# Encoder layer on one core: another tile order, squares ahead of high parts, and five smaller moves in the last two stages

## The reference

```python
o = rms_norm(o, sub_norm) * (1.0 - lam_init)
mix = jnp.concatenate([o_att * jax.nn.silu(g_att), o_lru * jax.nn.silu(g_lru)], axis=-1)
h = h + jnp.einsum('bsc,cd->bsd', mix, w_out[l])
e = jnp.einsum('bsp,pd->bsd', p[l], w_ple[l]) * jax.nn.sigmoid(jnp.einsum('bsd,de->bse', h, w_pg[l]))
h = h + rms_norm(e, g_ple[l])
```

## Time and profile before

| | us |
|---|---|
| times of three runs | 1026.09, 1027.68, 1029.20 |
| median | 1027.68 |
| profiled execution | 1027.9 |
| its span | 1026.1 |

### The profile page before, as it was taken

One profiled execution on the slowest core, in us unless ns is written; L12 is line 12 of the kernel. 1 busy time (PEld: TensorE's weight loads), 2 busy tenths in 40 slices (PEclk: granted clock), 3 DMA queues, 4 the chain that ended last, 5 costly groups with the idle time before them and its releaser, 6 DMA issues.

```text
span 1026.1 us, 15666 instructions
## 1 busy us (share of the span) xinstructions
PE 990.3 (97%) x5720; PEld 785.2 (77%) x5720; DVE 679.0 (66%) x1117; ACT 636.8 (62%) x1051; POOL 482.8 (47%) x396
## 2 busy tenths in 40 slices
PE   8999999999999999989999999999989999999996
PEld 7867777777788888878777777777767887777775
DVE  4735857592583341579999999999848672444444
ACT  7748485846631231569999999999737443444442
POOL 1163343626656540155677676665610125555451
PEclk9999999999999999999999999999989999999999
DMA  9741543323255437659867666523457780222221
GB/s 345 273 142 36 174 149 104 118 82 134 72 177 184 142 95 204 212 158 234 208 195 173 149 188 173 132 93 124 171 168 239 230 280 10 72 74 81 86 73 68
DMA packets 106909, 154.55 MB, mean 151 GB/s; under 512 B 10313, under 2 KB 69193, under 8 KB 106825
## 3 DMA queue, kind: packets, MB, share of 16 engines
q1 hardware_dynamic: 106688, 153.55, 50.0%
q10 hardware_dynamic: 144, 0.00, 0.0%
HBM read 104.17 MB, written 46.20 MB: 147 GB/s over the span
## 4 chain that ended last, share of the span: by engine, by line
PE 66%; DVE 17%; issue 10%; ACT 3%; POOL 2%; DMA 2%; DVEq 0%; POOLq 0%; SPq 0%; ACTq 0%
DVE E_ L1899 10%; PE b_ps L2340 6%; PE b_ps L2342 6%; PE b_ps L2341 6%; PE b_ps L2202 6%; PE b_ps L2204 5%; PE b_ps L2203 5%; PE o_ps L2397 3%; PE s_ps L2353 3%; PE w_ps L2314 3%; PE uT_ps L2277 2%; DVE ratio L1908 2%; PE left_ps L2527 2%; PE left_ps L2530 2%; PE left_ps L2529 2%
## 5 line engine op out<-in xcount | busy, mean ns | idle before, releaser
L1381 ACT ACTIVATE E_<-E_,nmax 128x1024 f32<-128x1024 f32 (+1 forms) x184 | 186.6, 1018 | 13.2 <-DVE nmax L1899 13.2
L1899 DVE CUSTOM_DVE_ANT_0 E_<-s_ps,bias 128x1024 f32<-128x1024 f32 (+1 forms) x184 | 188.2, 1057 | 9.2 <-PE s_ps L2353 9.0
L1087 POOL TENSOR_TENSOR E_<-E_,ratio 128x576 f32<-128x576 f32 (+3 forms) x92 | 84.7, 920 | 92.6 <-DVE E_ L1915 92.6
L1090 POOL TENSOR_TENSOR E_<-E_ 128x576 f32<-128x576 f32 (+3 forms) x92 | 103.6, 1126 | 7.2
L2204 PE MATMUL b_ps<-u_hi,wA_lo 128*128 128x512 f32 x256 | 99.8, 390 | 0.0
L2353 PE MATMUL s_ps<-KL,QL 128*128 128x512 f32 x256 | 88.6, 430 | 8.1 <-DVE nmax L1899 8.0
L1396 ACT ACTIVATE WT<-w_ps 128x1024 f32<-128x1024 f32 (+1 forms) x96 | 83.5, 870 | 5.9 <-PE w_ps L2314 5.5
L2314 PE MATMUL w_ps<-ident,E_ 128*128 128x128 f32 x624 | 83.5, 273 | 2.1 <-ACT WT L1396 2.0
L2202 PE MATMUL b_ps<-u_hi,wA_hi 128*128 128x512 f32 x216 | 85.5, 396 | 0.0
L2314 PEld LDWEIGHTS w_ps<-ident,E_ 128*128 128x128 f32 x624 | 72.5, 140 | 15.2 <-issue 6.3
L2203 PE MATMUL b_ps<-u_lo,wA_hi 128*128 128x512 f32 x216 | 84.1, 389 | 0.0
(11 more groups left out here) (345 smaller groups left out, 2595.8 us busy)
## 6 DMA issues: line engine op xcount, KB each, us to landing
QL<-qk_t SPq DMA_DIRECT2D x32, 256.0 KB, 7.2
KL<-qk_t SPq DMA_DIRECT2D x32, 256.0 KB, 8.5
bias<-line_d SPq DMA_DIRECT2D x8, 960.0 KB, 12.1
x_sb<-in_x SPq DMA_DIRECT2D x12, 512.0 KB, 9.0
z_ch<-z_stage SPq DMA_DIRECT2D x24, 256.0 KB, 3.2
qk_t<-qh SPq DMA_DIRECT2D x24, 256.0 KB, 2.3
qk_t<-ql SPq DMA_DIRECT2D x24, 256.0 KB, 2.8
mf<-mix_t SPq DMA_DIRECT2D x24, 256.0 KB, 4.8
```

Of the source, the lines that this page charges most:

```text
L1090: gp.tensor_tensor(one, one, two, ALU.add).then_inc(w_gp, 1)
L1381: act.activation(e, e, ACT.Exp, bias=nmax[:, n % 5, c:c + 1], scale=-1.0, accum_out=sums[:, n % 5, c:c + 1]).then_inc(e_done, 1)
L1899: dve.tensor_tensor_reduce(weights_at(n)[:, c, 0:n_tok], s_ps[:, c, 0:n_tok], b[:, ::-1], -1.0, 3e38, ALU.add, ALU.min, nmax[:, n % 5, c:c ...
```

## The change

It touches the tile loop and the pair loop alone.

- `SEQ`: tile 2 comes third and tile 8 fourth; `WHOLE` and `HALF` follow. Bank and waits are renumbered with it, and `add_x(3)` is done in two halves.
- SP: `load_o(2)` is issued ahead of the last `store_o`; in each step `load_mix(n + 2)` now stands ahead of `load_o(n + 3)`. The wait for the last `store_o` stands ahead of `load_o(3)`.
- ACT: in each step from the second on, `square_o(n + 3)` stands ahead of `mix_high(n + 1)`; `root_o` moves to just ahead of `scale_o` of the same tile. `gate_high` comes after both. The small instruction that had made the square root's table load early is dropped. The high parts of the embedding weights are made one step earlier.
- POOL: the first `wp_lo` ahead of the last `add_half`, the first three sums' low parts ahead of `p_low`.
- DVE: `mean_square(2)` ahead of `o_gate(1)`; `joined(g, 3)` ahead of `scaled_e(g, 1)`; in the last pair the multiplication by the gain writes to `sg` and needs only `e`, not its square, and the last additions are reordered.

```diff
-        SEQ = [0, 1, 8, 2, 9, 3, 10, 4, 11, 5, 6, 7]
+        SEQ = [0, 1, 2, 8, 9, 3, 10, 4, 11, 5, 6, 7]
...
             load_x_again(1)
+            load_o(2)
             store_o(1, HEADS // 2 - 1)
-            sp.wait_ge(o_st[1], 16 * 4)
-            load_o(2)
             load_mf(10)
             for n in range(NT):
+                if n + 2 < NT:
+                    load_mix(n + 2)
+                if n == 0:
+                    sp.wait_ge(o_st[1], 16 * 4)
                 if n + 3 < NT:
                     load_o(n + 3)
-                if n + 2 < NT:
-                    load_mix(n + 2)
...
             for k in range(1, len(HALF)):
+                if k == len(HALF) - 1:
+                    embedding_low(0)
                 add_half(k)
...
+            embedding_low(1)
...
+            sums_low(0)
             gp.wait_ge(fin["x_sum"], len(HALF))
             p_low(0, 1)
             p_low(0, 0)
-            sums_low(0)
...
             heads_out(2 * HEADS - 1)
+            square_o(2)
             mix_high(1)
-            act.activation(mse[:, 0:1], neghalf[:, 0:1], ACT.Sqrt, scale=-2.0)
-            square_o(2)
-            root_o(2)
...
             for n in range(NT):
+                if n == 0:
+                    root_o(2)
+                    scale_o(2)
+                if n + 3 < NT:
+                    square_o(n + 3)
                 if 1 <= n < NT - 1:
                     mix_high(n + 1)
-                if n + 2 < NT:
+                if 1 <= n < NT - 2:
+                    root_o(n + 2)
                     scale_o(n + 2)
-                if n + 3 < NT:
-                    square_o(n + 3)
...
             for g in range(PAIRS):
                 if g:
                     joined(g - 1, 3, "p2", right_ps[:], sg[0][:, LEFT])
+                    scaled_e(g - 1, 1)
                     gated_e(g - 1, 0)
...
                 a12_low(g + 1)
-                scaled_e(g, 1)
```

More of the change, by code:

```diff
@@ L459, in mix_bank @@
         def mix_bank(i):
-            if i < 3:
-                return (h_ps[:], hq_ps[:], all_ps[:, 4:8:3, :])[i]
+            if i < 4:
+                return (h_ps[:], hq_ps[:], h_ps[:], all_ps[:, 4:8:3, :])[i]
             return h_ps[:] if i % 2 else hq_ps[:]
@@ L1118, in add_half, with embedding_low @@
                                  ).then_inc(fin["x_sum"], 1)
+            def embedding_low(k):
+                gp.wait_ge(wp_hi_done, k + 1)
+                gp.tensor_tensor(wp_lo[:, k, :], wp_raw[:, k, :], wp_hi[:, k, :].bitcast(F32),
+                                 ALU.subtract).then_inc(wp_lo_done, 1)
             o_scale(0)
@@ L2010, in add_x @@
                     dve.wait_ge(fin[f"h_out{n % 2}"], 16 * min(n // 2, 4))
+                if n == 3:
+                    dve.tensor_tensor(h_sb[:, n, LEFT], mix_bank(n)[:, 0, :], row[:, LEFT], ALU.add)
+                    dve.tensor_tensor(h_sb[:, n, RIGHT], mix_bank(n)[:, 1, :], row[:, RIGHT], ALU.add
+                                      ).then_inc(fin["h_done"], 1)
+                    return
                 dve.tensor_tensor(h_sb[:, n % 4, :].rearrange("p (a b) -> p a b", a=2), mix_bank(n),
@@ L2063, in _ @@
             heads_scaled(2 * HEADS - 1)
+            mean_square(2)
             o_gate(1)
             mix_low(1)
-            mean_square(2)
             for n in range(NT):
@@ L2159, in half_gain @@
             def half_gain(k, r, c):
-                dve.wait_ge(fin["esq"], 2 * LAST + k)
-                dve.tensor_tensor(e_sb[:, r, c], e_sb[:, r, c], gpB[:, c], ALU.mult).then_inc(fin["t_done"], 1)
+                dve.wait_ge(fin["e_done"], START["e_done"] + 2 * LAST + k)
+                dve.tensor_tensor(sg[r][:, c], e_sb[:, r, c], gpB[:, c], ALU.mult).then_inc(fin["t_done"], 1)
             def last_mean(r, one, two):
@@ L2166, in last_mean, with last_sum @@
                                   ALU.add).then_inc(fin["ems"], 1)
-            def last_sum(r):
+            def last_sum(r, parts):
                 dve.wait_ge(fin["ers"], START["ers"] + 2 * LAST + r + 1)
-                for c in (RIGHT, LEFT):
-                    dve.scalar_tensor_tensor(out=e_sb[:, r, c], in0=e_sb[:, r, c], scalar=rse[:, r:r + 1],
+                for c in parts:
+                    dve.scalar_tensor_tensor(out=e_sb[:, r, c], in0=sg[r][:, c], scalar=rse[:, r:r + 1],
                                              in1=h_sb[:, slot_of(LAST, r), c], op0=ALU.mult, op1=ALU.add
@@ L2184, in _ @@
             dve.wait_ge(fin["t_done"], 2 * LAST + 3)
-            last_sum(0)
+            last_sum(0, (RIGHT,))
+            half_gain(4, 1, LEFT)
             last_mean(1, 1, 4)
-            half_gain(4, 1, LEFT)
+            last_sum(0, (LEFT,))
             dve.wait_ge(fin["t_done"], 2 * LAST + 4)
-            last_sum(1)
+            last_sum(1, (RIGHT, LEFT))
         @block.tensor
@@ L2470, in mix_product @@
                     pe.wait_ge(o_done, 2 * HEADS)
-                if n >= 3:
-                    pe.wait_ge(fin["h_done"], 1 if n == 3 else n - 1)
+                if n == 2 or n >= 4:
+                    pe.wait_ge(fin["h_done"], {2: 1, 4: 2, 5: 3}.get(n, n - 1))
                 if n in WHOLE[1:]:
```

4 lines of the change are left out of this document (1 added, 3 removed).

## The result

The changed kernel takes 1040.64 us, the median of four runs (1040.31 to 1042.75), beside 1027.33 us for the kernel before (1026.09 to 1029.2): a ratio of 1.013, with a 95% interval from 1.011 to 1.015. It is slower. Its profiled execution took 1040.31 us, its span 1038.5.

What follows compares the result with a forecast made beforehand. TensorE was taken as busy for 97% of the span, with a new load wait deciding the tile loop; +13.2 + 3.2 - 3.65 - 2.5 = +10.25 on 1027.9 gave 1038.15, said as 1038 us, range 1032 to 1046.

Steps and rivals of the forecast that it cites:

- The new wait: Tile loop, once per tile: ScalarE's square waits for the o_in load behind Gt's; period 9.65 us, where it was 7.08.
- L: Landing time of the o_in load issued behind Gt in the tile loop: 3.4 us taken, ends 2.8 and 5.0.
- the formula: Tile loop: the period from square to square is 6.25 + L us.
- The start, -2.6: Start of the tile loop: the third tile's turn comes 2.6 us early, at 762.4, since its load no longer waits.
- The sixth turn: Tile loop: the sixth tile's turn starts at 794.4, 8.2 us later than before.
- Short steps, +2.5 each: Two single-half tiles between the long ones in the tile loop: 8.55 us instead of 6.03, 2.5 us lost each.
- Clock, +3.2: TensorE idles ahead of three long tiles; two falls of the granted clock at 1.6 us taken, range 0 to 6.6.
- End of the tile loop, -3.65: Before the first p5: sums start earlier on GpSimd, 2.05 us of stall and 1.6 of clock dip won.
- Pairs, -2.5: Pair loop: joined(g, 3) ahead of scaled_e(g, 1) saves 0.5 us five times; other end 0, for the reload of h.
- the fourth: Rival for the whole kernel: the clock doesn't fall and the load is quick (2.8); -6.2, 1032 us; chance 0.1.
- The first: Rival for the whole kernel: the wait is hidden and all gains come; -11.8, 1016 us; chance 0.05.
- the signs named in advance: Profile: turns 9 to 10 us apart from the third, twelfth about 16 us later, no stall before any p5.

Runs made afterwards that it cites:

- e1: Changed kernel with mix_high(n + 1) ahead of square_o(n + 3) on ScalarE again, SyncE's order kept; 1027.41 us.
- e3: Changed kernel with both tile-loop orders, ScalarE's and SyncE's, as they were before; 1021.95 us.
- e7: Changed kernel with matmuls without use ahead of the third, fourth, fifth, eighth and tenth turns; 1039.93 us.
- e9: Changed kernel with matmuls without use ahead of the third, fourth, fifth, sixth, eighth and tenth turns; 1037.85 us.
- e8: Changed kernel with both tile-loop orders back, early table load, second wp_lo behind sums_low(0), gate_weights(n) ahead of mean_square(n + 3); 1018.05 us.
- e4: Changed kernel with SyncE's attention output load ahead of the gate's load, but behind the same wait for the gate's product; 1032.85 us.
- e6: Kernel before with one edit: VectorE's addition of p2 ahead of the scaling of e in the pair loop; 1023.81 us.
- after: The changed kernel itself, against the kernel before; 1040.64 us.
- e12: Changed kernel with both tile-loop orders back and gate_weights(n) ahead of mean_square(n + 3) on VectorE; 1020.78 us.
- e10: Changed kernel with the small square root put back on ScalarE between the first square and the second high part; 1041.76 us.

## Why the prediction was right

I had said 1038 (1032 to 1046) and slower with 0.92. Step by step, against the second turn:

- **The new wait.** Right in mechanism and place: idle times of 4.2 to 6.4 us before the squares of the ring, released by the load of `o_in`; e1 to e3 show that it takes both orders. Given L, the formula held within 0.06 us in seven of eight steps.
- **L.** 3.4 was taken, the five loads in the five places took 3.25, 5.27, 3.08, 3.15 and 4.53 us, 3.86 on average: 2.3 us more than counted. This was the largest error. The average lies inside the bounds of 2.8 and 5.0, the 5.27 alone outside. It isn't a constant of the kernel: the same five places took 3.2 to 4.9 us in e7.
- **The start, -2.6.** Too good: -1.4. The failing step is "I add 0.4 for VectorE, which sums the squares ahead of the gate of the second tile". VectorE lost 1.43 us there (the gated tile starts 2.06 us after the second turn, where 0.63 was needed), since the square's load, issued at 749.92 behind those of `mf` and `x_rd`, took 5.9 us and landed only after the turn began. What stood in a wait before was moved ahead of work that was ready. That the fourth turn still came 18.60 us after the second, where the sum had 18.62, is luck: the first load of the ring was issued 1.5 us later than counted (3.3 instead of 1.8 us after the second turn), took 3.0 us instead of 5.0, and its square then waited 0.7 us for ScalarE's scalings.
- **The sixth turn.** Counted from the second, 37.9 us worked out, 39.35 measured, above all by the one load of 5.27 us.
- **Short steps, +2.5 each.** +2.3 and +3.7; the second has the load of 4.53.
- **Clock, +3.2.** +3.3 (1.60 and 1.69), two falls, as taken. e7 and e9 confirm the price from the other side. The count is in part luck: TensorE was to idle 3.6 us before the sixth turn too and idled 0.68, since the tile before it ran at half the clock, which the sum hadn't thought of; e7, which keeps that clock up, has the idle time and the fall.
- **End of the tile loop, -3.65.** -2.7: 1.24 for the stall and 1.4 for the clock behind it. The failing step is "one `wp_lo` (2.4 of the 4.77) fills an idle time before the last `add_half`, and the sums start at about 852.75": GpSimd had come to it 0.8 us late, with an addition of 3.68 us ahead, and the second `wp_lo` still stood ahead of the sums. e8 has moved that, and its stall is 0.2 us.
- **Pairs, -2.5.** -3.0: a period fell from 27.36 to 26.64 us, 0.72 and not 0.5, since more went than the idle time that the row showed (between the last matmul of `p1` and the first of `p5` 0.24 instead of 0.91). The fifth gain was taken by the reload of `h`, which I had named as the other end.
- **Last pair, 0.** -0.1.

From the sum, +10.25, to the 12.4 of the span it is some 2.2 us: 2.3 for L, 1.0 for the end of the tile loop, 0.1 for the clock, less 0.5 in the pairs and 0.75 by which this execution reached the tile loop earlier; 0.1 is rounding.

Of the rivals, the fourth (no fall of the clock and a quick load, 1032) is near what e4 made, 1032.85 us, but in part by another way: e4 also takes the 0.42 us of the gate's issue out of five places, 2.1 us that the rival didn't count, and one of its loads took 4.73 us. The first, a hidden wait at 1016, didn't come; with the ring taken out, by e3, the rest of the change is worth 5.6 us, not 11.8, since the gain at the third turn is lost again in a ring of 7.3 us.

Of the signs named in advance two came out otherwise. Counted from the second turn, the twelfth stands 18.9 us later than before and not 16, with two steps of 11.5 us in the ring where 9 to 10 were named; and a stall is left before the first `p5`, 0.91 us.

## What to carry to other kernels

Before an instruction is put first on its engine, ask what releases it, and follow that back through the other queues: here an order on ScalarE and an order on SyncE, which cost 2.9 and 5.5 us alone, closed a ring through a transfer and cost 18.7 together. What the ring is longer than TensorE's own work, added up over its turns, was most of the loss, and the falls of the clock were the rest. Write such a ring as constants plus the transfer's time, L, and count how often L stands in the path, for its size is the least certain term. Where TensorE begins to stand still before a long run of matmuls, add the clock, and look for work that fits in the idle time.

## What the runs showed of the hardware

The fall of the clock is not a fixed function of the idle time before. 2.16 us of it were followed by the lower level of 1.2 GHz in the changed kernel (before the eighth turn) and in the kernel before (first `p5`). Nearly the same idle time at the same `p5` in e6 was followed by full speed, 2.4 GHz (first two rows). And before the fourth turn, behind the same twelve matmuls without use, 2.70 us in e7 were followed by the lower level and 2.85 us in e9 by full speed (last two rows):

```profile
857.38 0.50 PE L2527 MATMUL right_ps<-t_hi,s_hi 128*128 128x512 f32 x1 [2.12 <-POOL s_lo L1132]
858.30:861.50 3.20, 3.20 (x16) 2.56 (x15) 0.00 (x0) 0.60 (x1) 1.52 (x2) 1.00 0.00 0
775.87 0.66 PE L2482 MATMUL t_ps<-ident,O_n 128*128 128x128 f32 x4 [2.85 <-ACT O_n L1483]
775.90:779.00 3.10, 3.10 (x16) 2.61 (x17) 3.10 (x3) 1.73 (x1) 0.40 (x1) 1.00 0.44 177
```

Idle times of 1.28 and 1.54 us (e4) were not followed by a fall, those of 2.90 (e7), 3.54 (after) and 4.77 us (e12) were. So in this kernel an estimate may count on the price, 1.6 us for a long tile, but between 2 and 3 us of idle time not on whether it comes.

The loads of `o_in`, 256 KB each, took 2.6 to 2.9 us with nothing ahead in six of the eight that e4's loop issued behind its wait, and 3.9 and 4.7 in the other two. With the gate's load issued 0.42 us ahead, the eight of the changed kernel took 3.1 to 3.6 us in six cases and 4.5 and 5.3 in two. Which of them is slow differs between the profiled executions of the kernels that have this order: the slow ones took 5.3 and 4.5 us in the changed kernel, 4.9 in e7, 4.2 in e9, 5.6 and 5.2 in e10. The four times of e10 lie between 1038.1 and 1044.9 us; that the loads make this spread is likely, but not shown, since one of the four was profiled.
